# Chosen keys of the sample in fewer passes over 11 steps, and weights' signals regrouped, in a hybrid decoder step

## The reference

```python
_, idx = lax.top_k(sc, k_top)                       # mixer A: 256 of 2056 keys for a sample token
...
sv, si = lax.top_k(s, PEER_TOPK)                    # experts: 8 heads, 16 of 128 in each half
cv, ci = lax.top_k(cand, PEER_TOPK)
...
act = jax.nn.gelu(jnp.einsum('td,thkd->thk', xb, peer_u[e]).astype(jnp.float32))
return jnp.einsum('thk,thkd->td', (g * act).astype(xb.dtype), peer_v[e])
```

## Time and profile before

| what | value |
|---|---|
| time, median of 3 runs | 2349.43 us (2338.41 to 2356.35) |
| time of the profiled execution | 2348.06 us |
| its span | 2346.3 us |
| PE, DVE, ACT, POOL busy | 75%, 69%, 42%, 53% |
| bytes moved | 695.64 MB, 296 GB/s over the span |
| longest lines of the chain that ended last | TensorE L2230 8%, L2037 7%; VectorE L1690 6%; GpSimd L682 6% |

### The profile page before, as it was taken

How to read it: one execution, slowest core, us unless ns; L and a number is a source line. 1 busy time by engine, 2 the same in 40 slices (tenths; PEclk the granted TensorE clock), 3 DMA queues, 4 the chain that set the end, 5 groups by cost and what they waited for, 6 DMA issues and landing times.

```text
span 2346.3 us, 26214 instructions
## 1 busy us (share of the span) xinstructions
PE 1763.5 (75%) x8918; PEld 1299.5 (55%) x8918; DVE 1610.7 (69%) x3641; ACT 989.6 (42%) x1711; POOL 1234.0 (53%) x1251
## 2 busy tenths in 40 slices
PE   7995999638858967987877977847876976753556
PEld 3553657327646756665655755636654655543445
DVE  2546682887876777778676786786887778677441
ACT  1223343133544323555665664643342443233345
POOL 1000000367666666666667666656566656767664
PEclk9997799858977857978978987977987887875667
DMA  7001202499998989999999999979899889999997
GB/s 256 24 11 38 56 1 73 156 354 405 351 342 331 346 312 353 354 359 370 344 361 392 372 354 385 344 262 389 314 354 376 314 325 348 373 401 348 358 372 283
DMA packets 191573, 695.64 MB, mean 296 GB/s; under 512 B 26192, under 2 KB 28624, under 8 KB 188368
## 3 DMA queue, kind: packets, MB, share of 16 engines
q0 software_dynamic: 178608, 674.33, 76.2%
q1 hardware_dynamic: 12832, 19.65, 2.8%
HBM read 690.14 MB, written 3.76 MB: 296 GB/s over the span
## 4 chain that ended last, share of the span: by engine, by line
PE 42%; DVE 21%; issue 12%; POOL 6%; ACT 6%; another core or an unknown queue 5%; DVEq 4%; DMA 4%; ACTq 0%; POOLq 0%
PE ps L2230 8%; PE ps L2037 7%; DVE region L1690 6%; POOL region L682 6%; DVEq L1097 4%; DVE xall L1701 3%; DMA region<-in_peer_v,region 3%; PE ps L1722 2%; ACT region L1086 2%; PE ps L2054 2%; PE ps L1987 2%; PE ps L2130 1%; PE ps L2019 1%; PE ps L2082 1%
## 5 line engine op out<-in xcount | busy, mean ns | idle before, releaser
L682 POOL DMA_INDIRECT region<-in_peer_u,region x507 | 515.7, 1017 | 611.6 <-DVEq L1097 440.1
L2230 PE MATMUL ps<-ident,region 128*128 128x128 f32 x3312 | 552.7, 325 | 262.4 <-issue 138.1
L682 POOL DMA_INDIRECT region<-in_peer_v,region x571 | 571.7, 1001 | 335.2 <-issue 145.8
L1690 DVE SCALAR_TENSOR_TENSOR region<-region,h_now 128x1024 f32<-128x1024 f32 x507 | 611.7, 1214 | 116.5 <-DMA region<-in_peer_u,region 69.6
L2230 PEld LDWEIGHTS ps<-ident,region 128*128 128x128 f32 x3312 | 472.1, 169 | 350.6 <-issue 204.3
L1086 ACT ACTIVATE region<-region 128x1024 f32<-128x1024 f32 x414 | 464.9, 1139 | 245.0 <-DMA region<-in_peer_v,region 189.0
L2037 PE MATMUL ps<-w_uk_s,region 128*128 128x512 f32 x544 | 294.3, 669 | 8.7 <-issue 6.7
L1701 DVE SCALAR_TENSOR_TENSOR xall<-region,xall 128x1024 f32<-128x1024 f32 x157 | 201.7, 1285 | 20.9 <-issue 4.7
L2037 PEld LDWEIGHTS ps<-w_uk_s,region 128*128 128x128 f32 x544 | 106.3, 218 | 91.8 <-issue 88.2
L946 ACT ACTIVATE region<-ps 128x512 f32<-128x512 f32 x136 | 80.2, 590 | 163.5 <-PE ps L2037 101.3
L953 ACT ACTIVATE region<-ps 128x256 f32<-128x256 f32 x136 | 51.5, 379 | 202.2 <-remote 115.0
(11 more groups left out here) (404 smaller groups left out, 2824.5 us busy)
## 6 DMA issues: line engine op xcount, KB each, us to landing
region<-in_w_peer_q POOLq DMA_DIRECT2D x31, 512.0 KB
region<-in_peer_v,region POOLq DMA_INDIRECT x571
region<-in_peer_u,region POOLq DMA_INDIRECT x507
region<-in_w_in POOLq DMA_DIRECT2D x8, 882.0 KB, 14.8
region<-in_w_peer_q SPq DMA_DIRECT2D x8, 512.0 KB, 4.7
region<-in_x_turned SPq DMA_DIRECT2D x5, 512.0 KB, 3.5
region<-in_w_out SPq DMA_DIRECT2D x2, 1024.0 KB, 12.4
region<-in_w_out SPq DMA_DIRECT2D x1, 2048.0 KB, 18.3
```

Of the source, the lines that this page charges most:

```text
L682: pool.indirect_dma_start(ring[r][:], None, table, bass.IndirectOffsetOnAxis(ap=experts[:, t, n:n + 1], axis=0)).then_inc(landed[r], 16)
L1690: v.scalar_tensor_tensor(ring[r][:], ring[r][:], 1.0, h_now[:], ALU.mult, ALU.mult, accum_out=acts[:, t % 2, n:n + 1]).then_inc(S["u_done" ...
L2230: last = te.matmul(ps[6 + c // 4][:, (c % 4) * P:(c % 4 + 1) * P], ring[r][:, c * P:(c + 1) * P], ident[:], is_transpose=True, start=(m == ...
```

## The change

Three things. (1) `w_in`'s eight blocks signal in groups of 1, 2, 3 and 2 instead of four pairs; `g_cq`, which only ScalarE needs, has a semaphore of its own, and its load stands behind the one of the first tile, the identity's before it. (2) `chosen_keys()` counts with `scalar_tensor_tensor` and its accumulator over a broadcast column instead of comparing and then summing, and builds the mask from what is left out (`NONE`, -2^100) and the ties, so that the comparison "greater", two sums and the addition of the two masks go. (3) `sel` has its ten marks on steps 351 to 361, one to a step and the last on 360; `a_init`, `y1`, a0 to a7, `y2`, `lat`, `mixS`, `r4` and `c4` move five or six steps back: a0 began in step 361 and begins in 366, c4 ran in steps 493 to 506 and runs in 498 to 511.

```diff
@@ -37,6 +37,7 @@
 EPS = 1e-6
 NEG = -1e30
 TAKEN = -3e38
+NONE = -2.0 ** 100
 G = HA // KVA
 KTOP_P = min(256, SEQ // 4)
 KTOP_S = min(256, (PAST + NT) // 4)
@@ -262,7 +263,10 @@
 
         ident_in = sem("ident_in")
         g_mix_in = sem("g_mix_in")
+        g_cq_in = sem("g_cq_in")
         const_in = sem("const_in")
+
+        W_IN = [0, 1, 1, 2, 2, 2, 3, 3]
         w_in_in = [sem(f"w_in_in{i}") for i in range(4)]
         x0_in = sem("x0_in")
         x_in = sem("x_in")
@@ -361,6 +365,7 @@
 
         MB = 2 * (NPG + 4) + 15
         MA, MI, MR, MC, MX = 24, 8, 19, 34, 10
+        MK = 10
         C_PAGES = [(0, 6), (6, 12), (12, NPG + 1)]
         chain_b = [(f"b{b}", 36 + 55 * b, 36 + 55 * b + 50, MB) for b in range(NB)]
 
@@ -369,8 +374,8 @@
         chain_t = [("top", 166, 351, 2 * (NBIT + 1) + 4)]
         chain_a = [("c0b", 0, 36, MC), ("r1", 38, 54, MR), ("c1", 54, 98, MC), ("idx", 100, 160, NB * MI), ("rows", 160, 164, 6),
                    ("y0", 164, 167, 3), ("r2", 167, 184, MR), ("c2", 184, 244, MC), ("r3", 258, 275, MR), ("c3", 275, 351, MC),
-                   ("sel", 351, 356, 10), ("a_init", 356, 357, 2), ("y1", 357, 359, 3)]
-        at = 361
+                   ("sel", 351, 362, MK), ("a_init", 362, 363, 2), ("y1", 363, 365, 3)]
+        at = 366
         for b in range(NB):
             if b == NB - 2:
                 chain_a.append(("y2", at, at + 2, 3))
@@ -462,9 +467,9 @@
 
             load_xT(0)
             sp.dma_start(g_cols[:, 0:KD], a["g_norm_mix"]).then_inc(g_mix_in, 16)
-            sp.dma_start(g_cols[:, KD:], a["g_cq"]).then_inc(g_mix_in, 16)
+            sp.dma_start(ident[:], a["c_ident"]).then_inc(ident_in, 16)
             sp.dma_start(xall[:, 0, :], a["x_prompt"][0, 0:P, :]).then_inc(x0_in, 16)
-            sp.dma_start(ident[:], a["c_ident"]).then_inc(ident_in, 16)
+            sp.dma_start(g_cols[:, KD:], a["g_cq"]).then_inc(g_cq_in, 16)
             sp.dma_start(rope_a[:], a["c_rope_a"]).then_inc(const_in, 16)
             sp.dma_start(rope_b[:], a["c_rope_b"]).then_inc(const_in, 16)
             sp.dma_start(causal[:], a["c_causal"]).then_inc(const_in, 16)
@@ -487,7 +492,7 @@
             sp.dma_start(g_heads[:, 1, :], row("g_k_a", DH)).then_inc(const_in, 16)
 
 
-            sp.wait_ge(w_in_in[2], 32)
+            sp.wait_ge(w_in_in[2], 16 * W_IN.count(2))
             sp.wait_ge(xT_ready, 1)
             load_xT(1)
             sp.wait_ge(w_in_in[3], 32)
@@ -606,7 +611,7 @@
         def _(pool):
 
             for c in range(KD):
-                pool.dma_start(w_in[:, c, :], a["w_in"][c * P:(c + 1) * P, :]).then_inc(w_in_in[c // 2], 16)
+                pool.dma_start(w_in[:, c, :], a["w_in"][c * P:(c + 1) * P, :]).then_inc(w_in_in[W_IN[c]], 16)
             pool.dma_start(w_uq[:], a["w_uq"].rearrange("(c p) n -> p c n", p=P)).then_inc(weights_in, 16)
             pool.dma_start(w_uk[:], a["w_uk"].rearrange("(c p) n -> p c n", p=P)).then_inc(weights_in, 16)
             pool.dma_start(w_uv[:], a["w_uv"].rearrange("(c p) n -> p c n", p=P)).then_inc(weights_in, 16)
@@ -773,7 +778,7 @@
             act.wait_ge(x0_in, 16)
             x_square(0)
             x_scale(0)
-            act.wait_ge(g_mix_in, 32)
+            act.wait_ge(g_cq_in, 16)
             keep_projected(0)
             for t in range(NTILE - 1):
                 project(t)
@@ -1184,7 +1189,7 @@
                 settle()
                 v.tensor_tensor(qb[:], qb[:], g_qk[:, 0:1, :].broadcast_to([P, HB, DQK]), ALU.mult).then_inc(up_normed, 1)
 
-            dve.wait_ge(g_mix_in, 32)
+            dve.wait_ge(g_mix_in, 16)
             scale_x(0)
             x_norm(0)
             scale_x(1)
@@ -1557,14 +1562,17 @@
                 yield
 
             def chosen_keys():
-
-                greater, equal, order = (w[0:NTOK, :] for w in masks)
+                n = PAST + NT
+
+                left_out, equal, order = (w[0:NTOK, :] for w in masks)
                 first, second = t_two[0:NTOK, 0:1], t_two[0:NTOK, 1:2]
-                v.tensor_scalar(greater, scores, first, None, ALU.is_ge)
-                settle()
-                yield
-                v.tensor_reduce(trial_sum[0:NTOK], greater, AX, ALU.add)
-                settle()
+                one, none = t_pos[0:NTOK], t_sign[0:NTOK]
+                v.memset(one, 1.0)
+                v.memset(none, NONE)
+                settle()
+                v.scalar_tensor_tensor(order, scores, first, one.broadcast_to([NTOK, n]), ALU.is_ge, ALU.mult, accum_out=trial_sum[0:NTOK])
+                settle()
+                yield
                 v.tensor_scalar(t_two[0:NTOK, 2:3], trial_sum[0:NTOK], float(KTOP_S), None, ALU.is_ge)
                 v.tensor_scalar(t_two[0:NTOK, 3:4], trial_sum[0:NTOK], float(KTOP_S), None, ALU.is_lt)
                 settle()
@@ -1572,26 +1580,26 @@
                 settle()
                 v.scalar_tensor_tensor(first, second, t_two[0:NTOK, 3:4], first, ALU.mult, ALU.add)
                 settle()
-                yield
-                v.tensor_scalar(greater, scores, first, None, ALU.is_gt)
                 v.tensor_scalar(equal, scores, first, None, ALU.is_equal)
                 settle()
                 yield
-                v.tensor_reduce(trial_sum[0:NTOK], greater, AX, ALU.add)
-                settle()
-                v.tensor_scalar(trial_sum[0:NTOK], trial_sum[0:NTOK], -1.0, float(KTOP_S), ALU.mult, ALU.add)
-                yield
                 v.tensor_tensor_scan(order, equal, equal, 0.0, ALU.add, ALU.max)
                 settle()
                 yield
+                yield
+
+                v.scalar_tensor_tensor(left_out, scores, first, none.broadcast_to([NTOK, n]), ALU.is_le, ALU.mult, accum_out=trial_sum[0:NTOK])
+                settle()
+                v.tensor_scalar(trial_sum[0:NTOK], trial_sum[0:NTOK], 1.0 / NONE, float(KTOP_S - n), ALU.mult, ALU.add)
+                settle()
+                yield
                 v.scalar_tensor_tensor(equal, order, trial_sum[0:NTOK], equal, ALU.is_le, ALU.mult)
                 settle()
-                v.tensor_tensor(greater, greater, equal, ALU.add)
-                settle()
-                yield
-
-                v.tensor_scalar(i_row[0:NTOK, 0:PAST].rearrange("t (j p) -> t p j", j=PART), greater[:, 0:PAST].rearrange("t (p j) -> t p j", j=PART), -NEG, NEG, ALU.mult, ALU.add)
-                v.tensor_scalar(news, greater[:, PAST:PAST + NT], -NEG, NEG, ALU.mult, ALU.add)
+                yield
+
+                v.scalar_tensor_tensor(i_row[0:NTOK, 0:PAST].rearrange("t (j p) -> t p j", j=PART), equal[:, 0:PAST].rearrange("t (p j) -> t p j", j=PART), -NONE,
+                                       left_out[:, 0:PAST].rearrange("t (p j) -> t p j", j=PART), ALU.mult, ALU.add)
+                v.scalar_tensor_tensor(news, equal[:, PAST:PAST + NT], -NONE, left_out[:, PAST:PAST + NT], ALU.mult, ALU.add)
                 settle()
                 v.tensor_tensor(news, news, new_rows[:], ALU.add).then_inc(S["i_chosen"], 1)
                 yield
@@ -1800,7 +1808,7 @@
 
             pe.wait_ge(xT_ready, 1)
             for c in range(KD):
-                pe.wait_ge(w_in_in[c // 2], 32)
+                pe.wait_ge(w_in_in[W_IN[c]], 16 * W_IN.count(W_IN[c]))
                 for i, (c0, w) in enumerate(group_cols(DIN)):
                     last = te.matmul(ps[2 + i][:, 0:w], xT[:, 0, c, :], w_in[:, c, c0:c0 + w], start=(c == 0), stop=(c == KD - 1))
                     if c == KD - 1:
```

## The result

The changed kernel takes 2364.05 us (median of 20 runs) where the kernel before takes 2351.74 on the same chip: ratio 1.0055, 95% interval 1.0028 to 1.0082, so 13 us slower where +0.5 was predicted, and just above the range's upper end of 2364.

The account below looks back on a forecast made before the run. Time without transfers was taken to bound the kernel, 16.3 us of it at the chosen-key passes. Terms -11 (passes and spreading), +11.5 (move), 0 (start) gave +0.5, so 2349 us; range 2334 to 2364.

Parts of the forecast that it names:

- part 3: Attention a to c4 five steps later: costs 11.5 us, ceiling 15.6; moved page loads priced 0, 5 us either way.
- the stop: GpSimd standing before tile 4's first expert gather (step 512): forecast to grow from 6.4 to 22.0 us.
- part 2: Chosen-key passes over 11 steps instead of 5: 4.8 us from shorter waits plus 1.7 from freed slots.
- part 1: Chosen-key closing passes rewritten: 4.5 us of VectorE saved, all of it on the path.
- The two waits: VectorE's waits at the passes for ScalarE (3.33 us) and TensorE (6.20): half, 4.8 us, taken as saved.
- its floor: Least gain of parts 1 and 2 together: the 4.5 us of VectorE passes saved.
- the ceiling of 15.6: Highest cost allowed for the move: the whole growth of GpSimd's stop before tile 4, 15.6 us.
- Part 4: Start: TensorE's first matmul at about 9 us instead of 12.36, worth 0, bounds -0.6 and +1.0.
- Rival B: GpSimd's stop at step 512's gather costs all its growth, 15.6 us, as the queue empties early: 2359 us; chance 0.15.
- Rival A: Queue still deep at GpSimd's stop, dry time at the passes gone entirely: -9 us, 2339 us; chance 0.17.
- three tests set beforehand: Wrong if tile 4's stop is under 12 us, passes' dry time unmoved, or 1596 to 2066 changes over 8 us.
- the stretch between: From the passes to tile 4's choice (1596 to 2066 us): forecast not to change by more than 8 us.

Follow-up runs that it names:

- e_pass: Kernel before with only the new `chosen_keys()` passes, on the old five steps: 2134.16 us, ratio 0.9980.
- c_after2: The changed kernel again, unaltered, on a faster chip: 2149.27 us, ratio 1.0055 to the kernel before.
- f_mid: Changed kernel with passes in 6 steps (351 to 357), attention a and all behind it at their old steps: 2133.84 us, ratio 0.9965.
- f_r4mid: Changed kernel with passes in 8 steps, a_init at 359, a0 from 364, r4 in 7 steps: 2344.10 us, ratio 1.0002.
- e_start: Kernel before with only the start's part (w_in signals, g_cq semaphore, load order): 2140.64 us, ratio 1.0001.
- e_sel9: Changed kernel with passes in 9 steps (351 to 360), a_init at 360, the rest as changed: 2146.63 us, ratio 1.0036.
- f_mid2: The kernel of f_mid again, on a slower chip: 2345.65 us, ratio 0.9988 to the kernel before.
- e_tail5b: e_tail5 again, on another chip: 2368.37 us, ratio 1.0085 to the kernel before.
- e_c4late: Kernel before with c4 alone five steps later: 2149.43 us, ratio 1.0063.
- e_tail5: Kernel before with lat, mixS, r4 with its weights' loads, and c4 five steps later: 2362.96 us, ratio 1.0048.
- f_midtail5: f_mid with lat, mixS, r4, their loads and c4 five steps later: 2362.74 us, ratio 1.0057 to the kernel before.
- e_sel7: Changed kernel with passes in 7 steps (351 to 358), a_init at 358, the rest as changed: 2160.40 us, ratio 1.0095.

## Why the prediction was wrong

Two terms of the sum failed, by 5.5 and by 7 us and in the same direction: part 3's cost of the move (11.5 predicted, 17 measured), which counted only the stop and put everything else that moves at 0, and part 2's gain (11 together with part 1 predicted, 4 measured), which took it that time freed at the passes reaches the end.

**Part 1** was right in size. Saved 19.9 - 16.4 = 3.5 us of VectorE by the rows (4.5 priced, though its own terms, 19.9 - 15.1 - 0.2, give 4.6; the last pass is the difference), -4.3 us by e_pass (-7.7 to -1.1). The last pass could have been priced at 3.4 from L1593, which took 1.06 us more on those views than the comparisons do.

**Part 2 failed** where it took local gains for gains of the whole. The two waits fell from 9.5 to 4.3 us, more than the half that was priced, and the dry time beside the passes fell from 16.3 to 6.5 us, and to 37.8 x 0.17 = 6.4 in c_after3. But steps 351 to 384 together took 135.0 us before, 141.0 in the profiled change, and 37.8 + 98.0 = 135.8 in c_after3, whose two windows are

```profile
1534.00:1571.80 37.80, 24.26 (x126) 18.17 (x127) 34.17 (x49) 13.33 (x17) 29.79 (x20) 0.78 0.83 286
1571.80:1669.80 98.00, 66.20 (x351) 49.97 (x350) 58.79 (x87) 31.31 (x68) 55.25 (x57) 0.78 0.90 355
```

VectorE gets through steps 351 to 362 faster, TensorE starts a0's transposes 8.80 us late for want of the page, and VectorE then waits 15.35 us for attention a's first scores. I priced the chain behind the passes as work that only moves, and the page loads at zero. The distance in steps is not the reason: with four steps f_mid did not wait, with five f_r4mid waited 13.23 us. In the seven traces in which TensorE waited for this page it came 10.5 to 12.7 us behind its issue. Before, TensorE got to its transposes 12.43 us behind the issue and did not wait; in the change it got there 2.1 us behind it. On the faster chips the gain is not all gone at step 384: steps 351 to 384 take 120.1 us in e_start, 118.4 in e_pass, 113.0 in c_after2 and 107.5 in e_sel9, whose page wait is 1.22. So there 7.1 us of the 11 are won, and 12.6 without the late page.

The sum of both parts comes out as the change less the tail: (1.0056 - 1.0072) x 2352 = -4 us, within some 7 us either way (1.0056 is the mean of the changed kernel's two ratios on chips of this kind, 1.0072 of the three measurements of the tail, the closer ones weighing more). Predicted -11, which stands at the very edge of that; its floor, -4.5, is close to the value.

**Part 3** had the right mechanism and place. The stop was 20.1 us (22.0), the growth of the dry time 13.0 (11.5 priced). Mis-sized was the whole term: the tail costs 0.0072 x 2352 = 17 us, within some 5 either way, which is above the ceiling of 15.6, and in all six traces steps 480 to 512 grew by more than that ceiling (16.5 to 21.7). lat, mixS and r4 with its loads, which moved too, were priced at nothing; with c4 alone late the ratio gives 13.5 (9 to 18) and the trace 8.9, so 3.5 to 11 us are theirs. What among them costs it stays open beyond the 4 us argued for the loads.

**Part 4** was right: 0. TensorE did start at 8.95.

**The sum** is then -4 + 17 + 0 = +13 instead of +0.5. The -4 was found as the rest, so this sum checks nothing. Parts measured each against the kernel before do, if loosely: on chip 1 f_mid2's -2.8 us (0.0012 x 2352.6) and e_tail5b's +20.0 make +17.2 where the change stands at +13.4 (7 to 20), on chip 13 e_pass's -4.3 and e_c4late's +13.5 make +9.2 where it stands at +11.8 (7 to 16). The step from passes over 6 steps to 11 is in neither. What is shown is that the move of the tail decides: done alone it costs 11 to 20 us (e_tail5, f_midtail5 against f_mid2, e_tail5b), and where the tail stays, in f_mid, the kernel is 7.5 us faster than before (0.0035 x 2140.5); but how much of the missing 12.5 us is part 2's and how much part 3's is known only to about 7 us. Rival B named the place that decided, and its 2359 is nearest; it decided, as B said, by how soon the queue runs dry, though 4 us into the stop, not 2. Rival A fell with the 0.02 share in the stop. Of the three tests set beforehand the stop (over 12 us) and the dry time at the passes (moved) came out as forecast; the stretch between did not stay within 8 us: steps 362 to 480 took 449.9 us against 425.3, and in steps 362 to 384 alone the dry time grew by 11.7.

e_sel7 is slower than both its neighbours, with 9 and with 11 steps, by 0.4 to 0.6%, and its trace has the place: steps 351 to 384 take 120.9 us, 13.4 more than in e_sel9 (the medians differ by 13.8), beside GpSimd's two stops of 7.88 and 6.64 us. Open stays why those stops come with 7 steps, and what share of the whole kernel's time the late page takes: e_sel9 and c_after2 ran on different chips. f_mid, the best kernel, keeps passes and start and spreads by one step: 0.9965 on one chip, and 0.9988, no difference that can be measured, on the other kind.
